# The beginning of a two-layer encoder step, in another order

## What is computed

```python
def rmsnorm(x, g):
    xf = x.astype(jnp.float32)
    y = xf * lax.rsqrt(jnp.mean(xf * xf, axis=-1, keepdims=True) + EPS)
    return (y * g.astype(jnp.float32)).astype(x.dtype)
...
        h = rmsnorm(x, prm['ln_mix_pre'][i])
...
    qa, ka, va, fa, qb, kb, vb = split_cols(h @ w_in, ATT_SIZES)
```

## Time and profile before

| | before |
|---|---|
| median of 3 runs (1070.33 to 1070.6) | 1070.4 us |
| span of the profiled execution | 1068.7 us |
| TensorE busy | 1058.1 us (99%) |
| VectorE, ScalarE, GpSimd busy | 671.2, 537.2, 226.5 us |
| units 0 and 1 begin on TensorE | 14.84 us |
| unit 2 begins | 22.09 us |
| first scores begin | 40.91 us |
| first weights are turned | 47.35 us |

### The profile page before, as it was taken

How to read it: one execution, slowest core, us unless ns; L and a number is a source line. 1 busy time by engine, 2 the same in 40 slices (tenths; PEclk the granted TensorE clock), 3 DMA queues, 4 the chain that set the end, 5 groups by cost and what they waited for, 6 DMA issues and landing times.

```text
span 1068.7 us, 20366 instructions
## 1 busy us (share of the span) xinstructions
PE 1058.1 (99%) x7347; PEld 1042.5 (98%) x7347; DVE 671.2 (63%) x1236; ACT 537.2 (50%) x916; POOL 226.5 (21%) x355
## 2 busy tenths in 40 slices
PE   8999999999999999999999999999999999999998
PEld 8889999999999999999999999999999999999998
DVE  6876557777777753333977665657777777433365
ACT  5465465555455543333756545645555555433344
POOL 4500033222322320001310102222223322110000
PEclk9999999999999999999999999999999999999999
DMA  9622253555555545544454344365555555545532
GB/s 243 186 73 86 89 158 97 168 157 160 154 149 146 155 144 156 149 147 147 131 158 128 100 127 128 91 142 167 164 157 143 151 155 144 153 145 154 157 100 70
DMA packets 281926, 150.38 MB, mean 141 GB/s; under 512 B 5593, under 2 KB 278817, under 8 KB 281873
## 3 DMA queue, kind: packets, MB, share of 16 engines
q1 hardware_dynamic: 279184, 144.20, 48.3%
q0 software_dynamic: 2544, 5.40, 1.6%
q10 hardware_dynamic: 144, 0.05, 0.0%
HBM read 145.54 MB, written 4.08 MB: 140 GB/s over the span
## 4 chain that ended last, share of the span: by engine, by line
PE 93%; ACT 2%; DVE 2%; issue 1%; DMA 1%; POOL 1%; SPq 0%; DVEq 0%; POOLq 0%; ACTq 0%
PE bank L666 27%; PE bank L668 27%; PE bank L667 27%; PE bank L693 3%; PE bank L696 1%; PE bank L706 1%; PE bank L1037 1%; DMA raw<-in_w_att_in 1%; ACT wh L1186 1%; DVE wl L1490 1%; PE bank L939 1%; PE bank L722 1%; ACT S_sb L1207 0%; PE bank L900 0%; PE bank L1078 0%
## 5 line engine op out<-in xcount | busy, mean ns | idle before, releaser
L1490 DVE TENSOR_TENSOR wl<-raw,wh 128x1024 fp32r<-128x1024 f32 x270 | 332.4, 1232 | 251.0 <-ACT wh L1186 249.0
L666 PE MATMUL bank<-hH,wh 128*128 128x320 f32 x1280 | 399.8, 312 | 0.2
L668 PE MATMUL bank<-hH,wl 128*128 128x320 f32 x1280 | 395.9, 309 | 0.0
L667 PE MATMUL bank<-hL,wh 128*128 128x320 f32 x1280 | 395.8, 309 | 0.0
L1186 ACT ACTIVATE wh<-raw 128x1024 fp32r<-128x1024 f32 x270 | 284.4, 1055 | 177.1 <-PE bank L668 162.9
L666 PEld LDWEIGHTS bank<-hH,wh 128*128 128x128 f32 x1280 | 240.5, 188 | 1.3 <-issue 0.4
L667 PEld LDWEIGHTS bank<-hL,wh 128*128 128x128 f32 x1280 | 240.5, 188 | 0.2
L668 PEld LDWEIGHTS bank<-hH,wl 128*128 128x128 f32 x1280 | 240.4, 188 | 0.0
L666 PE MATMUL bank<-hidden_hi,wh 128*128 128x320 f32 x720 | 223.7, 311 | 0.5 <-ACT mix L1376 0.5
L667 PE MATMUL bank<-hidden_lo,wh 128*128 128x320 f32 x720 | 222.7, 309 | 0.0
L668 PE MATMUL bank<-hidden_hi,wl 128*128 128x320 f32 x720 | 222.7, 309 | 0.0
(11 more groups left out here) (371 smaller groups left out, 1027.4 us busy)
## 6 DMA issues: line engine op xcount, KB each, us to landing
raw<-in_w_ffn_up SPq DMA_DIRECT2D x128, 512.0 KB, 4.1
raw<-in_w_ffn_down SPq DMA_DIRECT2D x64, 512.0 KB, 3.9
raw<-in_w_rec_in SPq DMA_DIRECT2D x24, 512.0 KB, 3.9
raw<-in_w_att_in SPq DMA_DIRECT2D x18, 512.0 KB, 5.5
raw<-in_w_ple_gate SPq DMA_DIRECT2D x16, 512.0 KB, 4.0
raw<-in_w_att_out SPq DMA_DIRECT2D x8, 512.0 KB, 3.7
raw<-in_w_rec_out SPq DMA_DIRECT2D x8, 512.0 KB, 3.9
raw<-in_w_ple SPq DMA_DIRECT2D x4, 512.0 KB, 3.6
```

Source lines behind the costliest of these rows:

```text
L666: mmul(out, a, rh[:, k, :], start=first, stop=False)
L667: mmul(out, a, rl[:, k, :], start=False, stop=False)
L668: m = mmul(out, b, rh[:, k, :], start=False, stop=last)
L1490: V.tensor_tensor(wl[:, u % R, :], raw[:, u % R, :], wh[:, u % R, :].bitcast(F32), ALU.subtract).then_inc(lo_ready, 1)
```

## The change

The beginning of layer 0 stands in another order, on all engines; nothing is computed otherwise.

- The parameter transpose goes ahead of the x tiles. These use banks 4 to 7 in turn. VectorE copies the even tiles out of PSUM (`x_even`); ScalarE reads the odd ones there, for `hH`, and copies them too (`x_odd`).
- The products of constants between x tiles go. The hi x hi blocks 0 to 3 of unit 0 stand between tiles 4 to 7, and the rest of units 0 and 1 is ordered by the halves that it needs (`first_units`). Unit 2 runs its hi x hi blocks first (`unit_hi_first`).
- `stats` goes to unit 4 (behind 2 of 8 blocks) and `spread_rms` to unit 5 (behind 2). GpSimd adds the squares.
- Units 4 and 5 have banks 6 and 7 and run ahead of the cached keys; the first scores wait for their reads.
- ScalarE: `hi(0)` behind the first `hH`; `hi(4)` and `hi(5)` ahead of the narrow weights. VectorE: `lo(5)` behind the mean, `lo(7)` to `lo(9)` behind the first scores.
- The small loads are issued by SP, ahead of the loads of units 4, 6, 7 and 8.

```diff
-    e = [("cache", 4), ("u", 4), ("pe", 0), ("pe", 1), ("par", 0), ("u", 5),
+    e = [("u", 4), ("u", 5), ("cache", 4), ("pe", 0), ("pe", 1), ("par", 0),
...
-    o = [("x", 0), ("x", 1), ("par", 1)] + [("x", j) for j in range(2, KT)] + [("in0", i) for i in range(4)]
+    o = [("par", 1)] + [("x", j) for j in range(KT)] + [("in0", i) for i in range(4)]
...
+    fixed.update({("x", j): 4 + j % 4 for j in range(KT)})
+    fixed.update({("in0", 4): 6, ("in0", 5): 7})
...
+            def first_loads():
+
+                sp.dma_start(kcs[:], I["cache_swa_k"][0, 0].rearrange("p h d -> p (h d)")).then_inc(ld_band, 16)
...
+            def bias_loads():
+
+                sp.dma_start(kcache[:], I["cache_fox_k"][0, 0].rearrange("(t p) h d -> p t (h d)", p=P)).then_inc(ld_cache, 16)
...
+            def value_loads():
+
+                sp.dma_start(vcache[:], I["cache_fox_v"][0, 0].rearrange("(t p) h d -> p t (h d)", p=P)).then_inc(ld_cache, 16)
...
+            def parameter_loads():
+
+                sp.dma_start(prow[0:96, 1, :], I["ffn_conv_w"][1].rearrange("t (j c) -> (t j) c", c=P)).then_inc(par, 16)
...
+            beside = {R: first_loads, 6: bias_loads, 7: value_loads, 8: parameter_loads}
...
+                    if l == 0 and i in beside:
+                        beside[i]()
...
-            pool.wait_ge(raw_landed[2], 16)
-            pool.dma_start(kcs[:], I["cache_swa_k"][0, 0].rearrange("p h d -> p (h d)")).then_inc(ld_band, 16)
...
+            pool.wait_ge(sem("x_even"), KT // 2)
+            pool.wait_ge(sem("x_odd"), KT // 2)
+            g.memset(PTs[0:TS, P:3 * P], 0.0).then_inc(sem("PT_zero"), 1)
+            add_squares(pool, g, "mixpre0")
             inverse_rms("mixpre0")
-            pool.wait_ge(sem("x_in"), KT)
-            g.memset(PTs[0:TS, P:3 * P], 0.0).then_inc(sem("PT_zero"), 1)
-            pool.dma_start(kcache[:], I["cache_fox_k"][0, 0].rearrange("(t p) h d -> p t (h d)", p=P)).then_inc(ld_cache, 16)
...
+            pe.wait_ge(sem("ld_norms0"), 16 * 5)
+            parameters(1)
             pe.wait_ge(sem("ld_x"), 48)
-            for j in range(KT):
+
+            def turn_x(j):
+
                 gi = gid("x", j)
                 bank_free(pe, gi)
                 turn_rows(gi, T, lambda t: xtok[:, t, :], j)
-                if j == 1:
-                    pe.wait_ge(sem("ld_norms0"), 16 * 5)
-                    parameters(1)
-                if j >= 3:
-                    for i in range(3):
-                        mmul(bank[7][:, 0:P], ones[:], ident[:], start=True, stop=True)
+
+            def first_units():
+
+                out = [gbank(gid("in0", i))[:, 0:T] for i in range(FIRST)]
+
+                def hi_hi(i, k):
+                    if k == 0:
+                        bank_free(pe, gid("in0", i))
+                        pe.wait_ge(hi_ready, i + 1)
+                    pe.wait_ge(sem("h_hi"), k + 1)
+                    mmul(out[i], wh[:, i, k * P:(k + 1) * P], hH[:, k, :], start=k == 0, stop=False)
+
+                def lo_hi(i, k):
+                    if k == 0:
+                        pe.wait_ge(lo_ready, i + 1)
+                    mmul(out[i], wl[:, i, k * P:(k + 1) * P], hH[:, k, :], start=False, stop=False)
+
+                def hi_lo(i, k):
+                    pe.wait_ge(sem("h_lo"), k + 1)
+                    m = mmul(out[i], wh[:, i, k * P:(k + 1) * P], hL[:, k, :], start=False, stop=k == 7)
+                    if k == 7:
+                        m.then_inc(unit_used, 1)
+
+                for j in range(4):
+                    turn_x(j)
+                for j in range(4, KT):
+                    hi_hi(0, j - 4)
+                    turn_x(j)
+                for k in range(4):
+                    lo_hi(0, k)
+                for k in range(4):
+                    hi_lo(0, k)
+                for k in range(4):
+                    hi_hi(1, k)
+                for k in (4, 5):
+                    hi_hi(0, k)
+                    lo_hi(0, k)
+                    hi_hi(1, k)
+                for k in range(6):
+                    lo_hi(1, k)
+                for k in range(4):
+                    hi_lo(1, k)
+                for k in (6, 7):
+                    for i in range(FIRST):
+                        hi_hi(i, k)
+                        lo_hi(i, k)
+                for k in range(4, 8):
+                    for i in range(FIRST):
+                        hi_lo(i, k)
+
+            def unit_hi_first(u, out):
+
+                a, b = wh[:, u % R, :], wl[:, u % R, :]
+                pe.wait_ge(hi_ready, u + 1)
+                for k in range(8):
+                    mmul(out, a[:, k * P:(k + 1) * P], hH[:, k, :], start=k == 0, stop=False)
+                pe.wait_ge(lo_ready, u + 1)
+                for k in range(8):
+                    mmul(out, a[:, k * P:(k + 1) * P], hL[:, k, :], start=False, stop=False)
+                    m = mmul(out, b[:, k * P:(k + 1) * P], hH[:, k, :], start=False, stop=k == 7)
+                m.then_inc(unit_used, 1)
...
-                ahead([UNITS["in0"] + i for i in range(FIRST)], [gid("in0", i) for i in range(FIRST)], hH, hL,
-                      *prenorm_waits("mixpre0"))
-                in_unit(0, 2, lambda k: stats("mixpre0") if k == 5 else None)
-                in_unit(0, 3, rms_at("mixpre0", 6))
+                first_units()
+                bank_free(pe, gid("in0", 2))
+                unit_hi_first(UNITS["in0"] + 2, gbank(gid("in0", 2))[:, 0:T])
+                in_unit(0, 3)
...
+                        in_unit(0, i, {4: lambda k: stats("mixpre0") if k == 2 else None, 5: rms_at("mixpre0", 2)}.get(i))
...
+                        pe.wait_ge(sem("in_read0"), 6)
...
-                    act.wait_ge(sem("x_in"), j + 1)
                     if j == 0:
                         act.wait_ge(sem("par_in"), 1)
-                    A(hH[:, j, :], xT[:, j, :], ACT.Copy, scale=NC[:, 0, 64 + j:65 + j]).then_inc(sem("h_hi"), 1)
+                    gi = gid("x", j)
+                    if j % 2:
+                        bank_full(act, gi)
+                        x_tile = gbank(gi)[:, 0:T]
+                    else:
+                        act.wait_ge(sem("x_even"), j // 2 + 1)
+                        x_tile = xT[:, j, :]
+                    A(hH[:, j, :], x_tile, ACT.Copy, scale=NC[:, 0, 64 + j:65 + j]).then_inc(sem("h_hi"), 1)
+                    if j % 2:
+                        A(xT[:, j, :], gbank(gi)[:, 0:T], ACT.Copy).then_inc(sem("x_odd"), 1)
+                    if j == 0:
+                        hi(0)
                     if j == 3:
                         hi(1)
                 hi(2)
+                hi(4)
+                hi(5)
...
-                for i in range(4):
-                    hi(i + R)
+                hi(6)
+                hi(7)
...
-            hi(0)
...
-                    V.tensor_copy(xT[:, j, :], gbank(gi)[:, 0:T]).then_inc(sem("x_in"), 1)
-
+                    V.tensor_copy(xT[:, j, :], gbank(gi)[:, 0:T]).then_inc(sem("x_even"), 1)
...
+                par_in(1)
                 x_in(0)
-                x_in(1)
-                par_in(1)
                 x_in(2)
-                x_in(3)
+                h_low(0)
                 lo(0)
                 x_in(4)
-                x_in(5)
+                h_low(1)
+                x_in(6)
+                h_low(2)
+                h_low(3)
                 lo(1)
-                x_in(6)
-                prenorm_lo("mixpre0", 0, 0, 64)
-                x_in(7)
-                for j in range(1, 8):
-                    prenorm_lo("mixpre0", 0, j, 64)
+                for j in range(4, 8):
+                    h_low(j)
                 lo(2)
                 lo(3)
-                add_squares(dve, V, "mixpre0")
+                dve.wait_ge(sem("ld_band"), 16 * 3)
+                sink_rows(0)
+                sink_rows(1)
+                lo(4)
+                mean_square("mixpre0")
+                lo(5)
...
-                dve.wait_ge(sem("ld_band"), 16 * 3)
-                sink_rows(0)
-                mean_square("mixpre0")
-                lo(4)
-                sink_rows(1)
-                lo(5)
+                lo(6)
                 rms_rows("mixpre0")
-                in0_read(0)
-                in0_read(1)
-                in0_read(2)
-                lo(6)
-                in0_read(3)
-                lo(7)
+                for i in range(4):
+                    in0_read(i)
...
-                        lo(i + R)
+                        if i > 5:
+                            lo(i + R)
...
+                        if i == 0:
+                            for u in range(7, 10):
+                                lo(u)
```

More of the change, by code:

```diff
@@ L341, in encoder_step @@
             READ[gid("cache", i)] = ("cache_read", n + 1)
-        for name, signal, n in (("x", "x_in", 8), ("pe", "pe_f", 4), ("in0", "in_read0", 18),
+        for j in range(KT):
+            READ[gid("x", j)] = (("x_even", "x_odd")[j % 2], j // 2 + 1)
```

(19 more changed lines are left out.)

41 lines of the change are left out of this document (17 added, 24 removed).

## The result

The kernel after took 1074.56 us at the median of five runs, against 1070.4 before: ratio 1.0032 [1.0021, 1.0043]. Run again later, unchanged, it took 1072.6 at the median of seven, ratio 1.0024 [1.0012, 1.0036]. So it is slower by over 0.2%, where I gave that 25% and forecast 1071.3; the first median lies outside my range, the second inside, but only because the range reached up to rival A. Its runs stand in two groups: six from 1072.37 to 1072.95 and five from 1074.55 to 1075.54 (one more, 1145.73, fits neither and is left aside). There is a trace of each group, and what sets them apart is where TensorE's clock fell.

A forecast was written before the change was run, and what follows sets the result against it. TensorE's timeline was taken as the bound, each gap being program time, with VectorE's chain to the turned weights setting the end. 1070.4 plus a shift of 0.9 gave 1071.3 us, range 1069.5 to 1073.7.

The forecast's parts named there:

- rival A: At the start TensorE's clock falls to half rate: 2.2 us later on each mark, 1073.5 us; chance 21%.
- the sum: Whole kernel: the median before, 1070.4, plus a shift of 0.9 gives 1071.3 us; chance 58%.
- Turning x, the table load, the halves: Start: ScalarE's table load of 1.28 us comes onto the path at 9.97; first pass of unit 0 at 12.86.
- The third unit at 21.75: TensorE at the start: the third unit begins at 21.75 us, 0.34 earlier than before.
- the other 36 take 5.3: Units 0 and 1 on TensorE: after 12 of 48 passes at 16.45, the rest take 5.3 us, halves ready.
- Statistics, spread, adds on GpSimd: Units 2 to 5: GpSimd's adds end at 27, covered by statistics at 29.7; rstd is copied at 35.5.
- VectorE from rstd to the weights: VectorE's chain from 35.5 to weights turned at 48.1, with three wl costing 3.4; TensorE waits 2.4, not 0.41.
- 0.9 as the shift of all that follows: Behind the turned weights: everything comes 0.9 us later, as ScalarE's large copy at 46.12 moves by 0.9.
- Loads: GpSimd's 26 issues go to SP; unit 4's load, issued at 14.1, costs nothing, with 3.0 to 6.6 us of cover.
- No gap of this kernel this long shows a fall: Argument against a clock fall at the start, where TensorE has 2.6 us without work and then 2.4 thin ones.
- Rival C: Table load hidden, three wl find gaps: weights turned at 45.7 less 1.3, 2.9 earlier than before, 1067.5 us; chance 6%.

The follow-up runs named there:

- both repairs: Kernel after plus early table load, wl of unit 7 ahead of rstd, wl of 8 and 9 behind the read of unit 6: 1068.67 us, ratio 0.9984.

## Why the prediction was wrong, step by step

The step that failed is that the sum takes TensorE at full speed from beginning to end and gives the clock nothing but rival A's 21%. In every run of the kernel after the clock fell, at a price of 1.30 us in one trace and 2.70 in the other. The rest of the layout held to some tenths up to the turned weights: where the clock held, with products in the wait, three runs took the 1071.3 of the sum.

- **Turning x, the table load, the halves: right.** First pass 13.01 for 12.86; table load at 10.15 for 9.97. The page of the Trainium skill that I weighed (ScalarE: Activation LUTs, What ACT_TABLE_LOAD costs) adds a drain of 1.38 us; the rows show none, at either place of the load.
- **The third unit at 21.75: wrong in the run that I was to forecast, by 1.53.** The step that failed is "the other 36 take 5.3", at full clock. In the lower group they lost 1.30 to the clock. With the clock held, it takes 8.97 from the first pass to the third unit, where I had 8.89: 22.18 in the upper group, 21.63 with products in the wait.
- **Statistics, spread, adds on GpSimd: right in effect.** The adds ended at 28.50 (I had 27), the statistics waited for nothing.
- **VectorE from rstd to the weights: right.** 12.72 us for 12.6, a wait of 2.26 for 2.4.
- **"0.9 as the shift of all that follows": wrong.** In both groups a fall of the clock adds to it: 1.30 at the start, which moves the mark of the weights by 2.24 in all, or 2.70 behind the weights, whose mark has moved by 1.14.
- **Loads: right in the end, by a step that was wrong.** I took unit 4's load as issued at 14.1. SP's issues are not free: it was issued at 18.03, behind 11 small ones that began at 9.58, 8.45 us. The cover took it.

```profile
9.58 1.74 SPq L436 DMA_DIRECT2D kcs<-in_cache_swa_k  x1
...
18.03 1.05 SPq L430 DMA_DIRECT2D raw<-in_w_att_in  x2
```

- **Rival A: the right mechanism, with too low a chance and only one of its places.** I gave it 21% and 2.2 us, and asked what the clock does behind the wait at the start. I forecast a second wait of 2.4 us at 48 myself and didn't ask there. "No gap of this kernel this long shows a fall" was true because the kernel before has no wait over 0.9 us behind its warm-up; it was no evidence.
- **Rival C's mark came, but not its time.** With both repairs the weights are turned at 44.33, where C had 44.4, and 1.16 is given back behind them.

What stays open: why a run falls at the one place or at the other. The wait of 2.49 at the start brought the fall in one trace of after and not in the other, and the wait of 2.26 behind the scores likewise. By time and mean clock no run of after was without a fall, and two probably had both; no trace shows two. The Trainium skill (TensorE: Matmul & The Clock Gate, What's actually happening) says that the chip's look at activity runs free of the kernel's start, so that a change of level can land elsewhere from run to run. The two groups agree with that; no run here tests it.

## What to carry to other kernels

A new wait of TensorE costs more than its length: for every wait of the size seen here (2.3 to 4.9 us) that a change makes, give the clock a price, at each place. Shorter waits are not safe either: the clock fell behind 1.01 and 1.42 us in the kernel before without its fillers, and of three kernels whose longest wait behind the warm-up is 1.2 to 1.3 us in the trace, one, three and four runs in ten have a mean granted clock of 0.998. What looks like idle filling may be there for the clock; and filling that stands where the engine has since become the bound costs its own time. Work on a helper engine that nobody needs yet belongs behind what the critical engine waits for, and each time it is moved, look at what now stands behind it.

## What was not expected of the hardware

- A fall once begun lasts on, though TensorE is busy again: in the upper group the clock is at 0.50 from 50 to 56 us, and from 51.14 on TensorE works without a wait.
- Where GpSimd's adds and VectorE's work meet, one of the two is held up. In the kernel with both repairs wl of unit 3 took 1.77 and a copy of four columns up to 0.85; with the adds on VectorE 1.23 and 0.16. In the kernel after it was the add: wl of unit 3 took 1.22 from 21.58, and the add that began at 21.68 took 1.86. Its six adds took 0.87 to 1.86 each, not the 0.88 of the earlier trace rows. The Trainium skill (GPSIMD Engine Reference, Specifications) says that the two engines share their interfaces to SBUF, with contention when VectorE reads two inputs there or runs in a two-port mode. For wl, which reads two, the trace agrees; in which mode the copy ran, with its one input, no view shows.

```profile
21.58 1.22 DVE L1589 TENSOR_TENSOR wl<-raw,wh 128x1024 fp32r<-128x1024 f32 x1 [0.78 <-ACT wh L1270]
```

```profile
20.07 1.77 DVE L1591 TENSOR_TENSOR wl<-raw,wh 128x1024 fp32r<-128x1024 f32 x1 [1.07 <-ACT wh L1270]
21.76 0.85 DVE L1724 COPY sink<-sinkb 128x4 f32<-128x4 f32 x1
```

```profile
20.04 1.23 DVE L1590 TENSOR_TENSOR wl<-raw,wh 128x1024 fp32r<-128x1024 f32 x1 [1.07 <-ACT wh L1269]
...
24.57 0.16 DVE L1723 COPY sink<-sinkb 128x4 f32<-128x4 f32 x1
```

The first fence is the kernel after, the second the kernel with both repairs, the third that one with the squares on VectorE.
